# Cached keys of the streaming differential attention: loaded in the layout the scores read

## The reference, cut to what matters

```python
# cache_diff_k: (1, DEC_BATCH=8, PAST_LEN=512, B_HEADS=4, 2, HEAD_DIM=64), float32
def diff_core(q, k, v, mask, lam):
    s = jnp.einsum('bqhcd,bkhcd->bhcqk', q, k).astype(jnp.float32) * (HEAD_DIM ** -0.5)
    s = jnp.where(mask, s, -jnp.inf)
    p = jax.nn.softmax(s, axis=-1)
    a = p[:, :, 0] - lam * p[:, :, 1]
    return jnp.einsum('bhqk,bkhe->bqhe', a.astype(v.dtype), v)

def diff_sample(qb, kb, vb, ck, cv, lam):
    k_all = jnp.concatenate([ck, kb], axis=1)
    v_all = jnp.concatenate([cv, vb], axis=1)
    mask = jnp.ones((qb.shape[1], k_all.shape[1]), dtype=bool)
    return diff_core(qb, k_all, v_all, mask, lam)
```

## Time and profile before

| what | value |
|---|---|
| median of 3 runs | 1789.44 us |
| the profiled execution's own time | 1789.46 us |
| its span, first to last instruction | 1787.6 us |
| PE busy in the span | 1689.5 us (95%) |
| DVE, ACT, POOL busy | 1083.8, 721.8, 446.6 us |
| `kc_diff` transposes | 128 |
| ACT copies of them | 32 |
| mean granted TensorE clock | 0.989 |

### The profile page before, as it was taken

How to read it: one execution, slowest core, us unless ns; L and a number is a source line. 1 busy time by engine, 2 the same in 40 slices (tenths; PEclk the granted TensorE clock), 3 DMA queues, 4 the chain that set the end, 5 groups by cost and what they waited for, 6 DMA issues and landing times.

```text
span 1787.6 us, 30471 instructions
## 1 busy us (share of the span) xinstructions
PE 1689.5 (95%) x11585; PEld 1557.8 (87%) x11585; DVE 1083.8 (61%) x1930; ACT 721.8 (40%) x1439; POOL 446.6 (25%) x547
## 2 busy tenths in 40 slices
PE   7998989997898999989899999999999999999993
PEld 7997989876787999977799999999999999999982
DVE  6556555765456335224423677777777777777775
ACT  5123344576555123014302544444444444444443
POOL 2123321112222001100000133333333333333336
PEclk9999999999999999999999999999999999999997
DMA  6221322245575406337351011110111111111002
GB/s 232 98 78 56 95 79 87 78 160 175 180 240 192 161 25 229 114 132 255 110 187 48 25 48 48 47 44 27 46 47 47 47 47 47 47 47 43 27 12 106
DMA packets 106377, 170.35 MB, mean 95 GB/s; under 512 B 7416, under 2 KB 75640, under 8 KB 105240
## 3 DMA queue, kind: packets, MB, share of 16 engines
q1 hardware_dynamic: 78360, 126.78, 20.8%
q0 software_dynamic: 8160, 22.29, 3.7%
q10 hardware_dynamic: 19760, 19.92, 3.5%
HBM read 138.17 MB, written 31.72 MB: 95 GB/s over the span
## 4 chain that ended last, share of the span: by engine, by line
PE 87%; DVE 4%; ACT 3%; issue 2%; POOL 2%; DMA 2%; SPq 0%; ACTq 0%; DVEq 0%; POOLq 0%
PE banks L2178 26%; PE banks L2601 22%; PE banks L2611 19%; PE banks L2224 6%; PE banks L2379 2%; PE banks L2501 2%; PE banks L2166 2%; PE banks L2409 2%; PE banks L2449 1%; PE banks L2481 1%; PE banks L2320 1%; PE banks L2470 1%; ACT probs L1326 1%; POOL h L1105 1%; PE banks L2359 1%
## 5 line engine op out<-in xcount | busy, mean ns | idle before, releaser
L1105 POOL TENSOR_TENSOR h<-h,added 128x512 f32<-128x512 f32 x192 | 262.5, 1375 | 500.1 <-ACT added L1132 485.3
L2178 PE MATMUL banks<-w_hi,xt_hi 128*128 128x256 f32 x1224 | 355.6, 291 | 16.2 <-DVE xt_lo L1600 4.4
L2178 PE MATMUL banks<-w_hi,xt_lo 128*128 128x256 f32 x1224 | 345.0, 282 | 0.0
L2178 PE MATMUL banks<-w_lo,xt_hi 128*128 128x256 f32 x1224 | 344.8, 282 | 0.0
L2601 PE MATMUL banks<-xt_hi,w_hi 128*128 128x384 f32 x768 | 258.4, 336 | 0.0
L2601 PE MATMUL banks<-xt_hi,w_lo 128*128 128x384 f32 x768 | 258.2, 336 | 0.0
L2601 PE MATMUL banks<-xt_lo,w_hi 128*128 128x384 f32 x768 | 258.1, 336 | 0.0
L2178 PEld LDWEIGHTS banks<-w_hi,xt_hi 128*128 128x128 f32 x1224 | 233.5, 191 | 23.8 <-issue 8.9
L2072 DVE TENSOR_TENSOR h<-h,banks 128x512 f32<-128x512 f32 x304 | 206.1, 686 | 75.7 <-PE banks L2611 73.5
L2178 PEld LDWEIGHTS banks<-w_lo,xt_hi 128*128 128x128 f32 x1224 | 233.7, 191 | 0.0
L2178 PEld LDWEIGHTS banks<-w_hi,xt_lo 128*128 128x128 f32 x1224 | 233.4, 191 | 0.0
(11 more groups left out here) (268 smaller groups left out, 3316.2 us busy)
## 6 DMA issues: line engine op xcount, KB each, us to landing
w_raw<-in_w_up SPq DMA_DIRECT2D x16, 1024.0 KB, 5.4
w_raw<-in_w_down SPq DMA_DIRECT2D x16, 1024.0 KB, 4.9
w_raw<-in_w_xkv ACTq DMA_DIRECT2D x8, 1024.0 KB, 6.3
kc_diff<-in_cache_diff_k SPq DMA_DIRECT2D x16, 512.0 KB, 5.6
vc_diff<-in_cache_diff_v SPq DMA_DIRECT2D x8, 1024.0 KB, 5.4
w_raw<-in_w_in ACTq DMA_DIRECT2D x7, 1024.0 KB, 5.5
scaled<-mix_d SPq DMA_DIRECT2D x9, 512.0 KB, 5.5
h_d<-h SPq DMA_DIRECT2D x1, 4608.0 KB, 15.2
```

The source lines that it names most:

```text
L1105: pool.tensor_tensor(dst, dst, added[:, n % 2, :], ALU.add).then_inc(s_padd, 1)
L2178: last = mm(out, xt[:, k, tok:tok + P], w[:, k, :], start=(k == 0 and n == 0), stop=(k == KD - 1 and n == 2))
```

## The change

The host lays the cached keys out once, as (stream, feature within head, head, position), in the same way as it already did for the keys of the cross attention. One DMA of 1024 KB per stream then lands in the tile that the scores read. There are three such buffers: the two old ones and the space of `kc_diff`. All 32 `kc_diff` preps go, with their transposes and copies.

```diff
-for _b in range(DECB):
-    for _g in range(4):
-        PREP[STEP_NO[DIFFS[_b]] - (3 if _b >= 1 else 2) + _g // 2].append((("kc_diff", 4 * _b + _g), 7))
...
-        ktc_diff = [ktc_b[:, p] for p in range(2)]
+        ktc_diff = [ktc_b[:, 0], kc_diff, ktc_b[:, 1]]
...
-            def load_stream_keys(b, half):
-
-                if b >= 1:
-                    sp.wait_ge(s_prep, PREP_NO[("kc_diff", 4 * b - 4 + 2 * half + 1)] + 1)
-                rows = slice(2 * half * P, 2 * half * P + 2 * P)
-                sp.dma_start(kc_diff[:, 2 * half:2 * half + 2, :],
-                             a["cache_diff_k"][0, b, rows].rearrange("(t p) h c d -> p t (h c d)", p=P))\
-                    .then_inc(s_kd[half], 16)
+            def load_stream_keys(b):
+
+                if b == 2:
+                    sp.wait_ge(s_prep, PREP_NO[("mem", 3)] + 1)
+                if b >= 3:
+                    sp.wait_ge(s_sc, H_AT[STEP_NO[DIFFS[b - 3]] + 1])
+                sp.dma_start(ktc_diff[b % 3], a["cache_diff_k"][b]).then_inc(s_kd[b % 3], 16)
...
-            load_stream_keys(0, 0)
-            load_stream_keys(0, 1)
+            load_stream_keys(0)
...
             for b in range(DECB):
-                if b + 1 < DECB:
-                    load_stream_keys(b + 1, 0)
-                    load_stream_keys(b + 1, 1)
-                load_stream_values(b)
+                if b == 0:
+                    load_stream_keys(1)
+                    load_stream_values(0)
+                    load_stream_keys(2)
+                else:
+                    if b + 2 < DECB:
+                        load_stream_keys(b + 2)
+                    load_stream_values(b)
...
-                elif what == "kc_diff":
-                    b, kb = divmod(k, 4)
-                    last = copy(ktc_diff[b % 2][:, :, kb * P:(kb + 1) * P], blocks)
...
-                elif what == "kc_diff":
-                    b_, kb = divmod(k, 4)
-                    if kb == 0:
-                        pe.wait_ge(s_kd[0], 16 * (b_ + 1))
-                    if kb == 2:
-                        pe.wait_ge(s_kd[1], 16 * (b_ + 1))
-                    blocks = [kc_diff[:, kb, P * x:P * (x + 1)] for x in range(4)]
...
                 if kind == "diffs":
-                    pe.wait_ge(*prepared(PREP_NO[("kc_diff", 4 * x + 3)]))
+                    pe.wait_ge(s_kd[x % 3], 16 * (x // 3 + 1))
+                    pe.wait_ge(*prepared(PREP_NO[("k8", 0)]))
...
-                            mm(s[32 * hd:32 * hd + 32, 0, 0:PAST], zd[:, x, hd, :], ktc_diff[x % 2][:, hd, :],
+                            mm(s[32 * hd:32 * hd + 32, 0, 0:PAST], zd[:, x, hd, :], ktc_diff[x % 3][:, hd, :],
...
+    given["cache_diff_k"] = np.ascontiguousarray(
+        given["cache_diff_k"][0].reshape(DECB, PAST, 4, P).transpose(0, 3, 2, 1))
```

More of the change, by code:

```diff
@@ L118 @@
     _free = 3 if _kind == "diffs" else 1 - _i % 2 if _t < 4 else 7
-    PREP[_i] = [(what, _free if n % 2 and what[0] in ("kc_diff", "mem") else bank) for n, (what, bank) in enumerate(PREP[_i])]
+    PREP[_i] = [(what, _free if n % 2 and what[0] == "mem" else bank) for n, (what, bank) in enumerate(PREP[_i])]
 PREP_LIST = [(i, what, bank) for i in _ORDER for what, bank in PREP[i]]
@@ L387, in build @@
         s_q8 = sem("s_q8")
-        s_kd = [sem("s_kd0"), sem("s_kd1")]
+        s_kd = [sem(f"s_kd{i}") for i in range(3)]
         s_vd = sem("s_vd")
```

## The result

Five runs of the changed kernel had a median of 1780.06 us (1777.77 to 1783.74), five of the kernel before beside them 1792.61 (1787.69 to 1795.37); the ratio is 0.9937, with an interval of 0.9918 to 0.9956. The forecast was 1773.0 with a range of 1767 to 1780: the direction was right, the time 7 us too low. A repetition gave 1779.32 against 1790.32 us.

What follows compares the result with a forecast made beforehand. PE was taken to carry 87% of the chain, with waits deciding in some stretches. Terms summed to 17.7 us, the chain's pieces to 15.5 or 16.1; taking 16.5 gave 1789.5 - 16.5 = 1773.0 us, range 1767 to 1780.

Steps and rivals of the forecast that it cites:

- steps 40 to 43: Early steps: without key transposes, ACT's key copies and their bank waits, PE's work starts earlier; 5.1 us.
- 46 and 47: Steps where PE waits for `pick_c` anyway and the preps only filled the time; 0 us.
- (d): Rival, 400 to 485 us: more gaps on PE drop its clock to 1.2 GHz, 23 us lost, 1812; chance 0.03.
- Steps 51 and 52: PE's bank 7 waits for key preps go; DVE's list carried forward puts step 52's projection tile at 478.5; 4.1 us.
- upper bound: Whole change: all 128 transposes, all 6.2 us of idle ahead of them and step 52's clock fall; 22.6 us.
- step 48: The first prep's wait for a copy on bank 7 goes, with both preps' own time; 1.8 us.
- step 45: Holds a projection tile and PE doesn't wait in it, so the preps' time is won; 0.9 us.
- steps 53 to 57: Eight preps in steps 53, 54, 56 and 57 on a PE without gaps; 4.1 us.
- (a): Rival: in steps 40 to 43, 51 and 52 DVE and ACT still decide; only 8.5 us, 1781; chance 0.10.
- (b): Rival: the streams' value loads become late, three or four streams losing about 4 us, 1777; chance 0.07.
- (c): Rival: more than forecast, terms at their ends, clock fall gone, exponentials earlier; 22 us, 1767.5; chance 0.12.
- several falls of the clock: One of the signs listed beforehand that would show the forecast wrong; no size given.

Runs made afterwards that it cites:

- e4: Changed kernel with only the 8 preps of steps 53, 54, 56 and 57 put back as idle work nobody reads: median 1781.40 us.
- e7: Changed kernel with 74 idle matmuls ahead of PE's waits in 17 places: 1773.08 us, against 1779.32 for the changed kernel.
- e9: Kernel before the change with 76 idle matmuls ahead of its own PE waits: time not given, 1.8 us lost at equal clock.
- e10: Changed kernel with one weight unit's low half moved to the end of DVE's step 52, plus idle matmuls ahead of PE's waits: 1769.34 us.
- e11: Changed kernel with 74 idle transposes ahead of PE's waits in 17 places: 1771.98 us.
- e13: Kernel before the change with 76 idle transposes ahead of its own PE waits: 1786.84 us.
- e14: Changed kernel with one weight unit's low half moved to the end of DVE's step 52, plus idle transposes ahead of PE's waits: 1770.10 us.
- e15: As e14, with 73 more idle transposes at four more waits (steps 4 and 5, third output projection, cross attention): 1768.38 us.
- e12: As e10, with 73 more idle matmuls at four more waits (steps 4 and 5, third output projection, cross attention): 3.5 us slower than e10.

## Why the prediction was wrong

**The mechanism and the direction** were right. The loads cost nothing; the time is in the preps; in the early steps it is ACT's copies, in the last ones PE's transposes. With the clock held, steps 40 to 43 (5.1 forecast, 5.1 measured), 46 and 47 (0 and 0.1), 49 (0.2 and 0.1) and 50 (1.5 and 1.5) came out as worked out.

**The step that failed first: the clock, priced at nothing in the sum.** Rival (d) had the mechanism (gaps in PE's work lower the clock) but only as an all-or-nothing case at 0.03, and the sum carried no term for a little of it. Its "against" was one window of one profile, and the same kernel profiled again had 0.74 there. The changed kernel's mean clock is 0.9845 over 11 runs against 0.9874: 0.0028 x 1160 = 3.2 us. By the filled kernels it is 4 to 5. The profile I started from had a high clock, 0.989, though not a short time: its 1789.46 us is only 0.6 under the mean of the 68 runs. That the transposes' going is the cause is shown from both sides: put back, alone or with copies, they bring 0.9865 to 0.9878; others in the waits bring 0.9902. Only e4, the eight late pairs, where PE hardly waits, stays lower, at 0.9860.

**Steps 51 and 52** were 4.1 and measured 2.8 with the clock held, and this too is the clock. These are the scores of step 51 and the first matmul of the projection tile of step 52, before and after:

```profile
466.64 1.65 PE L2379 MATMUL banks<-heads_b 64*128 64x512 f32 x12
482.64 0.37 PE L2178 MATMUL banks<-w_hi,xm_hi 128*128 128x256 f32 x1
463.80 1.66 PE L2369 MATMUL banks<-heads_b 64*128 64x512 f32 x12
475.78 0.56 PE L2174 MATMUL banks<-w_hi,xm_hi 128*128 128x256 f32 x1
```

From one to the other it was 16.0 us before and is 11.98 now; the forecast's 478.5 makes it 11.9. So carrying DVE's list forward, with its split and the new waits, was right. But the 16.0 us hold the clock fall of step 52; in the filled kernel before, which has no fall, they are 14.4. The forecast named that fall's 1.5 us only in its upper bound, but the 482.6 that it subtracted from includes it; so its end was booked as won, and in the changed kernel a fall came back just behind the waits, in the tile: from the tile's start to the scores of step 53 it is 4.87 us, against 3.86 before.

**The term of step 48** was 1.8 and measured 0.9, that of 45 0.9 and 0.4. Both times the prep had stood between the scores and a values product whose turned probabilities were not there yet; with it gone PE waits 0.98 and 0.44 us for ACT. The forecast had looked for such a wait in step 46 and not in these two.

**The term of steps 53 to 57** was 4.1 and measured 3.6 with the clock held, 3.0 by idle preps. In step 53 the prep had covered a wait of 0.32 us for ACT's turned probabilities, which shows now; it is part of the missing time, and where the rest lies stays open.

**The balance.** Sum 17.7, with the clock held 14.4: of the 3.3 us between them 1.3 are steps 51 and 52, 0.9 is step 48, 0.5 step 45, 0.5 steps 53 to 57 and 0.1 step 49. I had taken 16.5. At the clock of 0.987 the change is worth 13.7; less 3.2 for the clock that is 10.5 us, the difference of the means (1790.1 and 1779.6). This last step proves nothing by itself, since the equal-clock figures are made from those means; the filled kernels are the independent measure. The forecast of 16.5 was thus 6 us too high: some 3 to 4 for the clock and the rest for the terms above.

**The rivals.** (a) is right only in part. With the clock held, steps 40 to 43 gave their whole term; in 51 and 52 DVE did go on to decide, as the sum already had it; the waits that took time back stood in steps 45, 48 and 53, which (a) doesn't name. (b) did not come: the values of streams 4 to 7 never wait. (c) did not come: 17.7 was an upper value, not a middle one. (d) came in small, and "several falls of the clock" was the one sign of being wrong that showed. The range reached down to (c) and up to (a), but not to a lower clock and a smaller sum together. 1780.06 lies 0.06 us outside it, and the repetition's 1779.32 inside: which side of the edge a median falls on is chance, the missing 6 us are not.

## What to carry to other kernels

Work removed from an engine's list opens a gap wherever the next instruction waits for another engine: check each such place by name, also those where the engine doesn't wait now. Don't book the end of a clock fall as won when the gap ahead of it stays. A gap on TensorE also costs clock, which one profile doesn't show; compare mean clocks over many runs, and put a term for it in the sum. If TensorE's waits can't be shortened, idle transposes cut to about 0.6 of each wait gave 7 us here, more than half as much as the change itself.

## What the runs showed of the hardware

- The mean granted clock goes with most of the spread between runs of one kernel: 1.16 us per 0.001 in the kernel before, 1.0 us left over. In the profiles of the kernel before, the time at the low level between 375 and 485 us was 3.4 us in one and 23.8 in another.
- Falls follow PE's waits: in the profile after, the five falls between 375 and 485 us come behind waits of 0.83, 0.92, 2.30, 0.73 and 1.80 us (ending at 380.6, 399.1, 410.0, 440.1 and 475.0); the wait of 0.98 us in step 48 is not followed by one, and what decides this stays open. With 17 or 18 waits filled, seven of the eight profiles (e7, e9, e10, e11, e13, e14, e15) have no fall from 375 to 485 us. The eighth, e12, has one, behind a wait for a DMA that nothing filled:

```profile
383.80 0.63 PE L2313 MATMUL banks<-ident,head_raw 128*128 128x128 f32 x4 [2.64 <-DMA head_v<-out_diff_v_prompt]
```

- Transposes kept the clock up as well as matmuls (0.9902 both).
- A float32 matmul of 128 by 128 by 128 leaves two rows and took 0.23 to 0.24 us in a row of them (35 in 7.98 us, 12 in 2.94), a transpose of the same tile one row and 0.11 to 0.13 (35 in 3.98, 12 in 1.53).
